# Query times state of each mLSTM chunk as three products of split, rounded operands, with the engines' calls around it in a new order

## The reference

```python
s = jnp.einsum("bhtd,bhsd->bhts", qq, kk) * w_intra
num = (jnp.einsum("bhts,bhsv->bhtv", s, vv)
       + w_inter[..., None] * jnp.einsum("bhtd,bhdv->bhtv", qq, C))
den = s.sum(-1) + w_inter * jnp.einsum("bhtd,bhd->bht", qq, n)
...
C_new = w_c[..., None, None] * C + jnp.einsum("bhs,bhsd,bhsv->bhdv", w_s, kk, vv)
n_new = w_c[..., None] * n + jnp.einsum("bhs,bhsd->bhd", w_s, kk)
```

## Time and profile before

| | us |
|---|---|
| median of 3 runs | 1395.86 (1394.98 to 1397.88) |
| profiled execution, its own time | 1396.0 |
| its span | 1394.1 |
| TensorE busy | 1381.7 (99%) |
| VectorE busy | 1163.3 (83%) |
| ScalarE busy | 765.6 (55%) |
| GpSimd busy | 154.6 (11%) |

### The profile page before, as it was taken

The page is one execution under the profiler, slowest core; times in us unless marked ns, Lnnn a source line. Parts: engine busy times, 40 slices in busy tenths (PEclk is TensorE's granted clock), DMA queues, the critical chain, the costliest instruction groups (busy, mean ns, idle before and its releaser), DMA issues.

```text
span 1394.1 us, 19118 instructions
## 1 busy us (share of the span) xinstructions
PE 1381.7 (99%) x6608; PEld 1156.3 (83%) x6608; DVE 1163.3 (83%) x1886; ACT 765.6 (55%) x1336; POOL 154.6 (11%) x250
## 2 busy tenths in 40 slices
PE   9999999999999999999999999999999999999997
PEld 7888888888888888888878888878888888888886
DVE  7989898898989989899774456797888888889976
ACT  6875766757665675767643336564333433346340
POOL 2002011110101111010000001001111111100021
PEclk9999999999999999999999999999999999999999
DMA  6114334252442525346497667434565556699661
GB/s 230 45 42 138 98 89 146 63 181 67 116 119 68 167 59 167 79 120 196 116 330 256 220 191 223 125 122 119 156 166 154 148 156 155 169 297 332 214 204 76
DMA packets 103439, 213.31 MB, mean 153 GB/s; under 512 B 10912, under 2 KB 27552, under 8 KB 102192
## 3 DMA queue, kind: packets, MB, share of 16 engines
q1 hardware_dynamic: 90544, 178.53, 38.0%
q0 software_dynamic: 12800, 33.56, 12.7%
HBM read 170.04 MB, written 75.56 MB: 176 GB/s over the span
## 4 chain that ended last, share of the span: by engine, by line
PE 70%; DVE 1%; POOL 0%; ACT 0%; issue 0%; DVEq 0%; POOLq 0%; ACTq 0%
PE wide L2926 14%; PE wide L2928 14%; PE wide L2927 14%; PE ps_state L2926 3%; PE ps_state L2928 3%; PE ps_state L2927 3%; PE ps_inter L2926 2%; PE ps_inter L2927 2%; PE ps_inter L2928 2%; PE ps_s L2926 2%; PE ps_intra L2926 2%; PE ps_intra L2928 2%; PE ps_s L2928 2%; PE ps_s L2927 2%; PE ps_intra L2927 2%; PE ps_intra L3106 1%
## 5 line engine op out<-in xcount | busy, mean ns | idle before, releaser
L2927 PE MATMUL wide<-xa,inb 128*128 128x512 f32 x576 | 224.8, 390 | 0.0
L2926 PE MATMUL wide<-xb,inb 128*128 128x512 f32 x472 | 189.9, 402 | 1.3 <-DVE inb L1936 1.1
L2928 PE MATMUL wide<-xb,inb 128*128 128x512 f32 x472 | 184.4, 391 | 0.0
L2927 PEld LDWEIGHTS wide<-xa,inb 128*128 128x128 f32 x576 | 108.4, 188 | 20.3
L2927 PE MATMUL wide<-xa,blk 128*128 128x512 f32 x320 | 124.5, 389 | 0.0
L2926 PEld LDWEIGHTS wide<-xb,inb 128*128 128x128 f32 x472 | 88.8, 188 | 20.0 <-DVE inb L1936 2.4
L2928 PEld LDWEIGHTS wide<-xb,inb 128*128 128x128 f32 x472 | 88.6, 188 | 19.2
L2928 PE MATMUL wide<-xb,blk 128*128 128x512 f32 x256 | 99.6, 389 | 0.0
L2926 PE MATMUL wide<-xb,blk 128*128 128x512 f32 x256 | 99.6, 389 | 0.0
L1855 ACT ACTIVATE wy<-wy_raw 128x1024 fp32r<-128x1024 f32 x56 | 59.4, 1062 | 61.7 <-DMA wy_raw<-y_block 61.5
L2926 PE MATMUL wide<-xa,inb 128*128 128x512 f32 x208 | 83.2, 400 | 0.6 <-DVE inb L1936 0.6
(11 more groups left out here) (449 smaller groups left out, 3959.0 us busy)
## 6 DMA issues: line engine op xcount, KB each, us to landing
in_raw<-in_w_in SPq DMA_DIRECT2D x45, 512.0 KB, 4.5
wy_raw<-y_block SPq DMA_DIRECT2D x56, 256.0 KB, 4.4
mw_raw<-h_block SPq DMA_DIRECT2D x53, 256.0 KB, 3.5
m_sum<-in_w_out POOLq DMA_DIRECT2D x48, 256.0 KB, 4.3
h_block<-f_buf SPq DMA_DIRECT2D x48, 256.0 KB, 4.3
w_sum<-in_pool_w_out POOLq DMA_DIRECT2D x48, 256.0 KB, 4.2
a_raw<-in_pool_w_z SPq DMA_DIRECT2D x16, 512.0 KB, 3.9
a_raw<-folded SPq DMA_DIRECT2D x16, 512.0 KB, 4.4
```

Source lines behind the costliest of these rows:

```text
L2926: pe.matmul(dst, a[0], b[0], start=first, stop=False, skip_group_check=more)
L2927: pe.matmul(dst, a[0], b[1], start=False, stop=False, skip_group_check=more)
L2928: return pe.matmul(dst, a[1], b[0], start=False, stop=last, skip_group_check=more)
```

## The change

Four things change together.

1. In each chunk from 1 to 7, TensorE forms query times state from split operands: hi x hi, hi x lo, lo x hi, with 258 columns (`state` gets one column more). ScalarE gets `round_q` (a 128x128 tile of `qw` into `qw_hi`, one buffer, so from chunk 2 on it waits for the chunk before) and `round_state` (`state` into `state_hi`); VectorE gets `low_q` (into `qw_lo`, which lies over `qw`) and `low_state` (`state_lo`). TensorE waits for `q_low` and `state_low` where it waited for `state_ready`.
2. `tanh_z` writes to one scratch, a half of `o_buf`, in all four steps; each step waits until the one before has been multiplied. `z_gate` is gone.
3. The calls of `first_half`, `second_half`, `next_head`, `first_layer_out` and `mix_tail` stand in a new order on both engines. A few calls before head 1 move too.
4. Near the end of the mixing, the steps on spare banks get other banks (`TAIL_BANKS`), and other `form_x` go to VectorE (`VECTOR_LATE`, `by_vector`). Four semaphores of the next layer are now the chunk's new ones, with an offset of 56.

The core of the diff, with ScalarE's and then VectorE's `first_half`; `second_half`, `next_head`, `first_layer_out` and `mix_tail` are reordered in the same manner.

```diff
+TAIL_BANKS = [*(b for i in range(4) for b in (0, *((1, 2, 3)[(4 * i + n) % 3] for n in range(4)))), 0, 2, 1]
+SPARE_BANKS = [i % 4 for i in range(len(SPARE) - len(TAIL_BANKS))] + TAIL_BANKS
+
+
 def spare_bank(step):
 
-    return SPARE.index(step) % 4
+    return SPARE_BANKS[SPARE.index(step)]
 
 
 def spare_prior(step):
 
     i = SPARE.index(step)
-    return SPARE[i - 4] if i >= 4 else None
+    return next((SPARE[k] for k in range(i - 1, -1, -1) if SPARE_BANKS[k] == SPARE_BANKS[i]), None)
 
 
 LEAD = 3
...
-VECTOR_LATE = (17, 19, 21, 23)
+VECTOR_LATE = (8, 10, 12, 14, 16, 18, 20, 22)
...
-    return n % 2 if n < 2 * KT else int(n in VECTOR_LATE)
+    return n % 2 if n < KT else int(n in VECTOR_LATE)
...
-            qw = sA("qw", [P, S])
+            with ExitStack() as whole:
+                qw = sA("qw", [P, S], F32, whole)
+            qw_lo = sA("qw_lo", [P, S], F32R)
...
-            state = sA("state", [P, DV + 1])
-            sA("line_s", [P, 31])
-            g_packed = sA("g_packed", [P, KT, 2 * HEADS])
-            z_gate = sA("z_gate", [P, HALF])
+            state = sA("state", [P, DV + 2])
             bias = sA("bias", [P, 1])
-            sA("line_b", [P, 15])
+            sA("line_s", [P, 29])
+            state_hi = sA("state_hi", [P, DV + 2], F32R)
+            sA("line_h", [P, 30])
+            state_lo = sA("state_lo", [P, DV + 2], F32R)
+            sA("line_l", [P, 30])
+            with ExitStack() as whole:
+                g_packed = sA("g_packed", [P, KT, 2 * HEADS], F32, whole)
+            qw_hi = sA("qw_hi", [P, P], F32R)
             sT_hi, kw_hi = (sA(name, [P, P], F32R) for name in ("sT_hi", "kw_hi"))
 
 
...
+        z_scratch = o_buf[:, 0, HALF:S]
...
-                if n >= 2:
-                    act.wait_ge(z_gated, 4 * h + n - 1)
-                elif n and h:
+                if n:
+                    act.wait_ge(z_gated, 4 * h + n)
+                elif h:
                     act.wait_ge(*h_stored(h - 1, 5))
-                elif h:
-                    act.wait_ge(z_gated, 4 * h - 1)
-                dst = o_buf[:, 0, half(1)] if n % 2 else z_gate[:, :]
-                act.activation(dst, z_buf[:, j, half(m)], ACT.Tanh, scale=0.5).then_inc(z_tanh, 1)
+                act.activation(z_scratch, z_buf[:, j, half(m)], ACT.Tanh, scale=0.5).then_inc(z_tanh, 1)
...
+            def round_state(h, c):
+                act.wait_ge(state_ready, (NC - 1) * h + c + 1)
+                act.activation(state_hi[:, :], state[:, :], ACT.Copy).then_inc(state_high, 1)
+
+            def round_q(h, c):
+                act.wait_ge(qw_ready, h + 1)
+                if c > 1:
+                    act.wait_ge(num_full, NC * h + c)
+                act.activation(qw_hi[:, :], qw[:, tile(c)], ACT.Copy).then_inc(q_high, 1)
...
             def first_half(h):
 
                 x = AT_A[3 * h + 2, 1] - 14
+                weighted_k(h - 1, 1)
                 take_num(h - 1, 0)
+                round_q(h - 1, 1)
+                round_s(h - 1, 1)
+                round_state(h - 1, 0)
                 tanh_z(h - 1, 2)
-                round_s(h - 1, 1)
-                weighted_k(h - 1, 1)
+                decay(h - 1, 2)
+                round_q(h - 1, 2)
+                weighted_k(h - 1, 2)
+                round_state(h - 1, 1)
                 take_num(h - 1, 1)
-                decay(h - 1, 2)
                 round_s(h - 1, 2)
                 decay(h - 1, 3)
-                weighted_k(h - 1, 2)
+                in_high(x + 5)
+                in_high(x + 6)
+                round_q(h - 1, 3)
+                round_s(h - 1, 3)
+                take_num(h - 1, 2)
+                round_state(h - 1, 2)
+                weighted_k(h - 1, 3)
+                round_v(h - 1, 1)
                 tanh_z(h - 1, 3)
-                weighted_k(h - 1, 3)
-                round_s(h - 1, 3)
+                decay(h - 1, 4)
+                round_q(h - 1, 4)
+                round_state(h - 1, 3)
+                take_num(h - 1, 3)
+                weighted_k(h - 1, 4)
+                round_s(h - 1, 4)
                 tanh_o(h - 1, 1)
-                take_num(h - 1, 2)
-                in_high(x + 5)
-                round_v(h - 1, 1)
                 tanh_o(h - 1, 2)
-                take_num(h - 1, 3)
-                decay(h - 1, 4)
...
-                t = o_buf[:, 0, half(1)] if n % 2 else z_gate[:, :]
-                dve.scalar_tensor_tensor(out=z_buf[:, j, half(m)], in0=t, scalar=1.0, in1=z_buf[:, j, half(m)],
+                dve.scalar_tensor_tensor(out=z_buf[:, j, half(m)], in0=z_scratch, scalar=1.0, in1=z_buf[:, j, half(m)],
...
+            def low_state(h, c):
+                dve.wait_ge(state_high, (NC - 1) * h + c + 1)
+                dve.tensor_tensor(state_lo[:, :], state[:, :], state_hi[:, :].bitcast(F32), ALU.subtract).then_inc(state_low, 1)
+
+            def low_q(h, c):
+                dve.wait_ge(q_high, (NC - 1) * h + c)
+                dve.tensor_tensor(qw_lo[:, tile(c)], qw[:, tile(c)], qw_hi[:, :].bitcast(F32), ALU.subtract).then_inc(q_low, 1)
...
-                    dve.tensor_copy(state[:, :], ps_state[:, 0:DV + 1]).then_inc(state_ready, 1)
+                    dve.tensor_copy(state[:, :], ps_state[:, 0:DV + 2]).then_inc(state_ready, 1)
                 else:
                     dve.scalar_tensor_tensor(out=state[:, :], in0=state[:, :], scalar=wc_bc[:, h * NC + c:h * NC + c + 1],
-                                             in1=ps_state[:, 0:DV + 1], op0=ALU.mult, op1=ALU.add
+                                             in1=ps_state[:, 0:DV + 2], op0=ALU.mult, op1=ALU.add
                                              ).then_inc(state_ready, 1)
...
             def first_half(h):
 
                 x = AT_A[3 * h + 2, 1] - 14
+                next_state(h - 1, 1)
+                in_sum(3 * h, 3)
+                low_k(h - 1, 2)
+                weighted_s(h - 1, 2)
                 gate_out_z(h - 1, 2)
-                weighted_s(h - 1, 2)
-                next_state(h - 1, 1)
                 low_s(h - 1, 2)
-                low_k(h - 1, 2)
-                in_join(3 * h - 1, 4)
-                in_sum(3 * h, 3)
-                weighted_s(h - 1, 3)
+                low_state(h - 1, 1)
+                low_q(h - 1, 2)
                 in_join(3 * h, 2)
                 chunk_stats(h - 1, 1)
-                low_s(h - 1, 3)
-                low_k(h - 1, 3)
+                weighted_s(h - 1, 3)
                 next_state(h - 1, 2)
-                in_low(x + 5)
+                low_q(h - 1, 3)
                 y_factor_o(h - 1, 0)
                 y_factor_f(h - 1, 0)
+                low_s(h - 1, 3)
+                low_state(h - 1, 2)
+                low_k(h - 1, 3)
+                in_join(3 * h - 1, 4)
+                chunk_stats(h - 1, 2)
                 next_state(h - 1, 3)
+                gate_out_z(h - 1, 3)
                 weighted_s(h - 1, 4)
-                gate_out_z(h - 1, 3)
-                y_factor_o(h - 1, 1)
+                low_q(h - 1, 4)
+                in_low(x + 5)
+                low_k(h - 1, 4)
                 low_s(h - 1, 4)
-                low_k(h - 1, 4)
-                chunk_stats(h - 1, 2)
+                low_state(h - 1, 3)
                 chunk_stats(h - 1, 3)
                 scales(h - 1, 0)
+                chunk_stats(h - 1, 4)
+                next_state(h - 1, 4)
+                low_k(h - 1, 5)
                 weighted_s(h - 1, 5)
+                y_factor_o(h - 1, 1)
+                low_s(h - 1, 5)
+                low_q(h - 1, 5)
+                low_state(h - 1, 4)
+                in_low(x + 6)
                 y_factor_f(h - 1, 1)
-                next_state(h - 1, 4)
-                low_s(h - 1, 5)
-                low_k(h - 1, 5)
-                in_low(x + 6)
-                y_factor_o(h - 1, 2)
-                chunk_stats(h - 1, 4)
                 next_state(h - 1, 5)
...
-                    pe.wait_ge(state_ready, (NC - 1) * h + c)
-                    mm = pe.matmul(ps_intra[:, 0:DV + 1], qw[:, tile(c)], state[:, :], start=False, stop=True)
+                    pe.wait_ge(q_low, (NC - 1) * h + c)
+                    pe.wait_ge(state_low, (NC - 1) * h + c)
+                    pe.matmul(ps_intra[:, 0:DV + 2], qw_hi[:, :], state_hi[:, :], start=False, stop=False)
+                    pe.matmul(ps_intra[:, 0:DV + 2], qw_hi[:, :], state_lo[:, :], start=False, stop=False)
+                    mm = pe.matmul(ps_intra[:, 0:DV + 2], qw_lo[:, tile(c)], state_hi[:, :], start=False, stop=True)
```

More of the change, by code:

```diff
@@ L1542, in first_layer_out @@
                 weighted_k(last, 5)
+                round_state(last, 4)
+                round_q(last, 5)
+                decay(last, 6)
                 round_s(last, 5)
@@ L2225, in first_half @@
+                weighted_s(h - 1, 7)
                 y_factor_o(h - 1, 3)
-                y_factor_f(h - 1, 3)
-                in_join(3 * h, 5)
-                weighted_s(h - 1, 7)
```

(46 more changed lines are left out.)

423 lines of the change are left out of this document (229 added, 194 removed).

## The result

The changed kernel takes 1400.05 us (median of 10 runs, 1399.17 to 1401.59) where the kernel before took 1396.14 in runs beside it (10 runs, 1394.98 to 1398.27). The ratio is 1.0025, 95% interval 1.0015 to 1.0035: slower, by 2.1 to 4.9 us, outside the range of 1391 to 1398. Its profiled execution took 1399.19 us, 1397.4 of them the span; the span before was 1394.1, so the two traces hold 3.3 of the 3.9 us.

What follows compares the result with a forecast made beforehand. TensorE was taken as the bound: kernel length is the sum of its instructions plus 12.4 us idle. 1396.0 - 3.9 (products) + 1.0 (new waits) - 0.3 (re-won waits) = 1392.8 us, range 1391.0 to 1398.0.

Steps and rivals of the forecast that it cites:

- The sum on TensorE: Query times state, 56 chunks: three rounded products replace one f32 product, 0.07 us less each, 3.9 us gained.
- What it adds elsewhere: Rounding work per chunk with a state: VectorE 0.53 us more, 3.7 us a head; ScalarE 3.5 us a head.
- Is it late anywhere?: TensorE waits for chunk 6's `sT_lo` and the values' `xm_lo`: together 0.15 us a head, 1.0 us lost.
- The re-won waits: TensorE's existing waits for `inb` and `o_buf`: up to 1.9 us may come back, 0.3 us taken.
- The rest of the edits: Shared z gate scratch and mixing tail: 0 taken, at worst 0.2 us a head and 1 us.
- The tail: End of the layer's mixing, new banks and `form_x` shares: 0 taken, at worst 1 us.
- The z gate's scratch: Tanh steps sharing one scratch, each waiting for the previous multiplication: 0 taken, at worst 0.2 us a head.
- (a): Saving eaten by waits of 0.3 us or more a head, or last head and tail: 1394.8 us; 34 in 100.
- (b): VectorE becomes the bound in each head, 8.4 us added, 1400.5 us; with (c) 16 in 100.
- (c): The three products cost their operand loads, 0.56 us a chunk: 7.5 us slower, 1403.5 us; 2 in 100.

Runs made afterwards that it cites:

- order_alone: The changed kernel with the old float32 query-times-state product and without the four rounding steps, new order kept: 1399.85 us, ratio 1.0029 to the kernel before.
- best2: The changed kernel with four calls moved in each head, another last-head order, and the tail's order and banks as before the change: 1399.60 us, ratio 1.0019.

## Why the prediction was wrong

- **The sum on TensorE** was right: 0.07 to 0.09 us a chunk. By the rule of the Trainium skill ("TensorE: Matmul & The Clock Gate", section "Wait — 56ns, not 53.3ns?"), columns over 2.4 GHz plus 2.5 ns, the new products would be an estimated 110 ns apart. The trace doesn't agree: the changed kernel's own rows have 0.12 us too.
- **What it adds elsewhere** was right in size: 0.34 us for the state's rest by the trace, 0.33 forecast. VectorE was busy 95.3% of 100 to 660 us, forecast 96 to 97.
- **Is it late anywhere?** failed in size, and it is the first of two steps that turned the sign. I took 0.15 us a head; the late steps sum to 6.5/7 = 0.93 us a head, and 3.8/7 = 0.54 was lost net of what came back. The two places that I named were right, even in time: chunk 6's `sT_lo` was forecast for 0.1 us after TensorE could load it, and the values' `xm_lo`, forecast 0.1 later than before, ended at 484.61, 0.6 later. But I looked only at those two, and only chunk 6 was late for the reason given, the rests: order_alone has the values late without them. Chunk 1, whose rests stand in `next_head`, and the join ahead of the next pair's product cost as much. And each place costs twice, a late product and a longer step behind it: 0.18 and 0.29 us at my two, where 0.15 was taken for both.
- **The re-won waits**, 0.3, were sized from the wrong source. Of the waits of the earlier trace rows only 0.6 us (`inb` 0.4, `o_buf` 0.2) lie between 85 and 659 us; both are gone. By the starts the kernel before has 2.1 us of late steps there, most of them in no row, and 1.9 of it is gone. So more came back than I took. The 1.3 us of `inb` before 85 us, which I counted among what could come back, stays (1.2 to 2.4 us in the profiles of the kernels tried).
- **The rest of the edits** failed most. The z gate and the tail were put at 0, at worst 0.2 us a head and 1 us, and `first_layer_out` was not laid out at all: its new order stands in no term of the sum. It cost 3.1 us: 2.1 by its order alone, which order_alone shows, and about 1.0 with the rests, which is little more than the spread of this stretch. A chain of calls there had no cover: `unit_lo(4)` behind a state that needs TensorE, `mw_low(0)` of 1.2 us ahead of chunk 5's `sT_lo`. That the two kernels' lists differ there could be read from the order before any run.
- **The tail**: 0 forecast, 0.3 in the profiled run; not told apart from no difference.
- **The z gate's scratch**, 0: no wait of TensorE stands on it. It wasn't tried alone.
- **Rivals.** (a), the gain eaten, was right in kind for the heads. (b) gave the time, 1400.5, by VectorE as the bound in each head; it isn't that, since 13 us less of VectorE's work give back only 1.7. That its time came out near the measured 1400.05 is luck. (c) is out.

What stays open: the changed kernel's median is 0.9 us above its profiled execution, and its waits can't be placed there. Waits of 1.4 and 2.3 us for a folded weight stand at 807 and 810 us in the profiles of best2 and order_alone, and in no other one of more than 0.3 us; they may be part of it.

## What to carry to other kernels

When work goes onto an engine that is 91% busy, lay its new list against the times of every place that hands an operand to the bounding engine, the head's first chunk, the joins and above all the last, irregular iteration too: those that stand in another function are where the loss was. Put the calls that nobody waits for into the gaps where the engine waits for its own chain, and look afterwards at the distance of starts, since the list of waits had 2.4 us of new rows for 7.2 lost. If a change is worth its gain only in a tuned order, measure that order with the old work in it: it told in one run which places were late by order and which by load, once the starts were read head by head.

## What the hardware showed that I had not expected

Small waits leave no idle row. With 6.5 us of late steps up to 659 us, TensorE's busy time of 100 to 660 us was 559.32 of 560 us, as before with 2.1 us (559.34); only the starts tell. And VectorE's time has no fixed price: in one order, at 523 to 537 us busy of 560, a us of it gave back 0.13 us below the present load, where half of the late places hang on the order, and cost 0.7 above it.
